# Column orders in the products of two gated layers: the same numbers, streamed in another order

## The reference

```python
def swiglu(x, w_gate, w_up, w_down):
    return (jax.nn.silu(x @ w_gate) * (x @ w_up)) @ w_down

def second_block(x, meta_tokens, ffn1_norm, ffn1_w_gate, ffn1_w_up, ffn1_w_down, ...):
    h = jnp.concatenate([meta, x], axis=1)
    h = h + 0.5 * swiglu(rmsnorm_2(h, ffn1_norm[l]), ffn1_w_gate[l], ffn1_w_up[l], ffn1_w_down[l])
    ...
    h = h + 0.5 * swiglu(rmsnorm_2(h, ffn2_norm[l]), ffn2_w_gate[l], ffn2_w_up[l], ffn2_w_down[l])
    return rmsnorm_2(h, final_norm)[:, N_META:]
```

## Time and profile before

| | |
|---|---|
| Median of 3 runs | 911.59 us (911.44 to 911.89) |
| Span of the profiled execution, first to last instruction | 911.4 us |
| PE busy | 896.9 us (98% of the span) |
| DVE, ACT busy | 642.1 us (70%), 525.5 us (58%) |
| DMA | 157.63 MB, mean 173 GB/s |

### The profile page before, as it was taken

The page is one execution under the profiler, slowest core; times in us unless marked ns, Lnnn a source line. Parts: engine busy times, 40 slices in busy tenths (PEclk is TensorE's granted clock), DMA queues, the critical chain, the costliest instruction groups (busy, mean ns, idle before and its releaser), DMA issues.

```text
span 911.4 us, 18458 instructions
## 1 busy us (share of the span) xinstructions
PE 896.9 (98%) x7415; PEld 880.6 (97%) x7415; DVE 642.1 (70%) x1108; ACT 525.5 (58%) x869; POOL 4.7 (1%) x11
## 2 busy tenths in 40 slices
PE   8999999999999999999999999999999999999996
PEld 7997999999999999999999999999999999999996
DVE  6999888777557666666675547768669877677553
ACT  6897876676336655444444435545775664544452
POOL 1000000000000000000000000000000000000000
PEclk9999999999999999999999999999999999999999
DMA  9742335255765666555556565554425556665641
GB/s 307 239 166 97 139 121 181 93 186 193 251 189 177 200 204 185 171 173 171 181 174 199 168 177 161 158 169 130 148 70 186 186 185 196 201 194 195 212 138 47
DMA packets 110613, 157.63 MB, mean 173 GB/s; under 512 B 9917, under 2 KB 61249, under 8 KB 110401
## 3 DMA queue, kind: packets, MB, share of 16 engines
q1 hardware_dynamic: 109776, 155.19, 53.2%
q10 hardware_dynamic: 576, 0.73, 0.2%
q0 software_dynamic: 176, 0.53, 0.2%
HBM read 155.37 MB, written 1.05 MB: 172 GB/s over the span
## 4 chain that ended last, share of the span: by engine, by line
PE 90%; DVE 6%; ACT 2%; issue 1%; DMA 1%; SPq 0%; DVEq 0%; ACTq 0%
PE ps L1044 28%; PE ps L1046 28%; PE ps L1045 27%; DVE wl L1817 2%; PE ps L1127 1%; ACT wh L1383 1%; PE ps L1091 1%; DMA X<-d_x 1%; DVE S L2222 1%; PE ps L1301 0%; PE ps L1321 0%; DVE S L2068 0%; PE ps L1259 0%; DVE X L1981 0%; PE ps L1281 0%
## 5 line engine op out<-in xcount | busy, mean ns | idle before, releaser
L1817 DVE TENSOR_TENSOR wl<-raw,wh 128x1024 fp32r<-128x1024 f32 (+2 forms) x291 | 346.2, 1212 | 191.4 <-ACT wh L1383 191.2
L1383 ACT ACTIVATE wh<-raw 128x1024 fp32r<-128x1024 f32 (+2 forms) x291 | 298.2, 1046 | 186.8 <-PE ps L1046 186.3
L1044 PE MATMUL ps<-U,wh 128*128 128x256 f32 (+2 forms) x1392 | 397.5, 286 | 2.3 <-DVE wl L1817 2.3
L1046 PE MATMUL ps<-U,wl 128*128 128x256 f32 (+2 forms) x1392 | 390.9, 281 | 0.0
L1045 PE MATMUL ps<-UL,wh 128*128 128x256 f32 (+2 forms) x1392 | 390.4, 280 | 0.0
L1044 PEld LDWEIGHTS ps<-U,wh 128*128 128x128 f32 (+1 forms) x1392 | 262.2, 188 | 5.3 <-DVE wl L1817 3.2
L1045 PEld LDWEIGHTS ps<-UL,wh 128*128 128x128 f32 (+1 forms) x1392 | 262.5, 189 | 1.6 <-issue 1.0
L1046 PEld LDWEIGHTS ps<-U,wl 128*128 128x128 f32 (+1 forms) x1392 | 262.0, 188 | 0.0
L1044 PE MATMUL ps<-H,wh 128*128 128x256 f32 (+1 forms) x736 | 207.4, 282 | 0.1
L1046 PE MATMUL ps<-H,wl 128*128 128x256 f32 (+1 forms) x736 | 205.4, 279 | 0.0
L1045 PE MATMUL ps<-HLO,wh 128*128 128x256 f32 (+1 forms) x736 | 205.1, 279 | 0.0
(11 more groups left out here) (340 smaller groups left out, 784.2 us busy)
## 6 DMA issues: line engine op xcount, KB each, us to landing
raw<-w_ff SPq DMA_DIRECT2D x64, 512.0 KB, 4.5
raw<-ffn_w_gate SPq DMA_DIRECT2D x88, 256.0 KB, 3.6
raw<-ffn_w_up SPq DMA_DIRECT2D x88, 256.0 KB, 4.5
raw<-ffn_w_down SPq DMA_DIRECT2D x44, 512.0 KB, 4.6
raw<-w_in SPq DMA_DIRECT2D x40, 512.0 KB, 4.0
raw<-w_out SPq DMA_DIRECT2D x16, 512.0 KB, 3.6
raw<-wkv_x SPq DMA_DIRECT2D x8, 512.0 KB, 4.2
raw<-w_in SPq DMA_DIRECT2D x9, 256.0 KB, 3.0
```

The lines of the kernel that those rows point to most:

```text
L1044: e.matmul(out, sh, xh, start=(i == 0 and n == 0), stop=False)
L1046: mm = e.matmul(out, sl, xh, start=False, stop=(over and n == nk - 1))
L1383: e.activation(wh, raw, ACT.Copy).then_inc(*up("w_hi", v))
L1817: lo = e.tensor_tensor(wl, raw, wh.bitcast(F32), ALU.subtract)
```

## The change

A new function `in_order` gives a view of the same columns in another order. It is applied to both streamed operands and to the output, so each column lands in its old place in the bank. Number of instructions, operands, waits and loads stay as they are.

```diff
+def in_order(name, g, a):
+
+    n = a.shape[-1]
+    if name not in ("sw1", "sw2"):
+        return a
+    if g in (1, 7):
+        return a[:, ::-1]
+    if g in (2, 8):
+        return a.rearrange("p (l c) -> p l c", c=16)[:, ::-1, :]
+    if g in (3, 9) and n == T1:
+        return a.rearrange("p (q l c) -> p l q c", q=2, c=16)
+    if g in (3, 9):
+        return a.rearrange("p (q l c) -> p l q c", q=2, c=34)
+    if g in (4, 10):
+        return a.rearrange("p (q c) -> p q c", q=2)[:, ::-1, :]
+    if g == 5:
+        return a.rearrange("p (q c) -> p q c", q=4 if n == T1 else 2)
+    return a
...
             xh, xl = streamed(t, name, k, tag)
             out = ps[0:m, 0:xh.shape[-1]]
+            xh, xl, out = (in_order(name, g, a) for a in (xh, xl, out))
             sh, sl = wh[:, n, off:off + m], wl[:, n, off:off + m]
```

## The result

| | Before | After |
|---|---|---|
| Lowest of 20 runs each | 911.25 us | 916.47 us |
| Median of 20 runs each | 913.22 us | 918.74 us |
| Span of the profiled execution | 911.4 us | 914.9 us |

The changed kernel is slower by 0.62% (ratio 1.0062, 95% interval 1.0041 to 1.0083), about 5.7 us; the forecast said 915.8 against 911.59, a ratio of 1.0046, and its range up to 927.0 holds the 918.74 us measured. Both kernels' runs fall into a lower cluster (before: 911.3 to 914.0, after: 916.5 to 920.5) and one some 6 us higher (before: 917.4 to 920.9, after: 923.1 to 925.3), which makes the medians move with the share of each. The experiments show where the upper one comes from.

The account below looks back on a forecast made before the run. PE's streaming was taken to bound the kernel. Terms of 2.9 + 0 (`sw2`) and 1.0 + 0.3 (`sw1`) sum to +4.2 us, onto the median 911.59 giving 915.8 us; range 909.8 to 927.

Parts of the forecast that it names:

- What bounds the kernel: PE, busy for 98% of the span, bounds the kernel; each ns per product is worth 0.77 us per gated stage.
- the `sw1` terms: Changed groups of `sw1`: 1.8 ns more per product, 1.0 us for three orders and 0.3 us for second half first.
- The stall at 5 ns in `sw2`: Falling, falling runs and halves in turn in `sw2`: one stall of 5 ns per product, 576 products, 2.9 us.
- Second half first in `sw2`: Groups 4 and 10 of `sw2`, 192 products: one jump per product, 0 us, at most 1.0.
- their bound of 1.7: Upper end for the three orders in `sw1`: +3.0 ns per product, from the stretch with 126.7 ns, +1.7 us.
- The base: Whole kernel before: the median of the runs, 911.59 us, onto which the +4.2 us were added; the span was 911.4.
- No effect: Rival, both gated stages: order after a product's start doesn't matter, time stays 911.6 us within 0.2%; chance 0.25.
- Half rate for falling: Rival, groups 1 and 7 of both stages: falling products take twice their columns' time, 38.4 us, about 950; chance 0.15.
- Faster: Rival: all 768 changed products of `sw1` come down to 120.0 ns, `sw2` stays; -2.8 us, 908.8; chance 0.12.

Follow-up runs that it names:

- experiment 11: Kernel before with falling order in the first unit of `ff1a` group 1 and 21 more places of six products each; twelve runs at 911.5 to 913.8 us, ratio 0.9986.
- experiment 1: Kernel before with only operands or only output reordered, by group, in both gated layers; untimed; `sw2` falling: operands alone 117.8 ns, output alone 113.5.
- experiment 3: Kernel before with falling order in groups 1 to 10 of both gated layers and weights moved by 0 to 224 bytes; untimed; `sw2` 117.8 to 120.0 ns.
- experiments 1 and 2: Experiment 1, and the kernel before in plain order with gated layers' weights moved by 0 to 224 bytes; second untimed, `sw2` 117.8 to 120.0 ns.

## Why the prediction was right, and where not

*What bounds the kernel*: right. PE stayed busy without a hole, and the group sums of the trace, +5.43 us where +4.2 was forecast, are the time: 5.7 us by the ratio, 5.2 by the lowest runs. A stall per product by the order of reading held; that it also depends on what streamed before was missing. Of the 1.2 us that were missing, 1.1 lie in the `sw1` terms.

*The stall at 5 ns in `sw2`* for three orders: right for two. Falling and falling runs cost 4.4 and 4.6 ns, as the earlier trace rows had it. Halves in turn cost 6.7; that term was mis-sized by 0.3 us in 192 products, and why the order costs more is not shown. The price came from a stretch that was not what it was taken for: the products of the earlier trace rows ran in the slow one of two lasting spacings, and the four tiles just behind them, which had 117.8 as well, ran at 113.3 ns in experiment 11, with their operands where they had been. That this price fits falling columns was in part luck. The whole term: 2.9 us expected, 3.0 measured.

*Second half first in `sw2`*: 0 expected, +0.02 us per group.

*`sw1`*: the mis-sized term. Priced at 1.8 ns from group 0, so 1.0 + 0.3 us; measured +1.4 (falling), +4.6 (falling runs), +3.3 (halves), +3.0 ns (second half first), 2.4 us in all. Group 0's mean was not the nearest row; its worst stretch, 126.7 ns, which I had kept as the bound, was nearer for three of four orders, and falling runs (128.3) and halves in turn (127.0) went past it. The three orders together cost 1.8 us, just over their bound of 1.7.

*The base*: the span of 911.4 us was not 0.2 us under the median of the runs. The profiled execution after has 914.9 us of span in a run of 916.71, 1.8 us around it, so the one before was a run of about 913.2. The chosen base of 911.59 is the lower cluster, and by it the sum fits. Of the 2.9 us from 915.8 to the measured median of 918.74, 1.6 are this base (913.22 over twenty runs), the rest the size of the change.

*Rivals.* "No effect" fell in eight groups of `sw1`, six of `sw2`. "Half rate for falling" fell: 117.8 ns. The rule of the Trainium skill that went with it (Advanced Engine Details and Errata, PSUM Cachelines) would have made the writes the cost; in experiment 1 they cost 0.1 to 0.6 ns a product in `sw2`, for three patterns that are not contiguous, so for this output format the measurement decides against it. No order here parts the two columns of a pair in the output, so what that costs stays open. Half rate exists, on the other side: 230 ns where every second column is read from SBUF. "Faster" fell: no order and no move took `sw1` below 123.6. The Trainium skill's rule of two independent read ports, by which loading weights takes nothing from the running product (TensorE: Matmul & The Clock Gate, Part 2), does not cover what is seen: with columns in plain order, moving the weights took the products that stream meanwhile from 113.3 to as much as 120.0 ns.

Not foreseen was that the order of the groups counts. In the change each group of falling runs is followed by halves in turn, which swap the slow spacing back to the fast one before plain groups come. That was luck: with one group of falling runs alone, 1392 plain products behind it paid 6.2 us.

## To carry to other kernels

Read the cost of back-to-back products from the distance of their starts, by stretch, and compare equal shapes: two lasting values for one instruction, here 113.3 and 117.8 ns, are a loss that no busy share shows. Stream columns in rising order, and keep the places at which the spacing is lowest; here seven of nine moves of the weights alone brought `sw2` to 118.3 ns or more. If runs of a kernel come in two clusters, compare the spacings of a stage in a trace of each; a few products in an order that always ends in the fast spacing can pin it down, but test that from both spacings, since an order that leads back from one may lead away from the other.

## What the runs showed of the hardware

A product of float32r with 256 columns at the granted 2.4 GHz ran at 113.3 or at 117.8 ns with the same addresses and the same order, and kept either for over a thousand products, until something else streamed. With 272 columns the plain groups of `sw1` showed one value only, 123.6 to 123.8. Falling columns (117.8 while they last) ended in the fast spacing from both; falling runs of 16 ended in the slow one; halves in turn swapped them; second half first kept what it found. These ends are from three to seven cases each (halves in turn from fast to slow: two), with the weights in their usual place; with the weights moved by 48 bytes, falling ended in the slow one (`dn2` at 117.8 in experiment 3). In the slow spacing of plain columns one weight load in three took 192 ns and the others 188. That reads of stream and weights collide in SBUF is inferred from experiments 1 and 2 (the order of reading and the place of the weights each change the spacing); which part they share, and what sets the offset at the start, stays open.

Behind an unlike product the spacing can come out either way with the same code: in `ff1a`, of the twelve traces whose code is the same up to the end of group 0, nine left the float32 products of line 1074 in the fast spacing and three in the slow one, which decided over 6.4 us of the 911. In group 0 of `sw2` all fourteen traces left them in the fast one. These two ways out of line 1074's products in `ff1a` make the two clusters in which this kernel's runs lie.
